# A hybrid decoder layer on one core: the opening's adaLN product in eight strips of one feature slice each

## The chip, the core and the metric

The kernel runs on 1 core of one Trainium2 chip. The metric is the time of one execution on the device, in microseconds (us). Before the change three runs took 726.54, 726.90 and 729.52 us: median 726.9 us.

## The reference

One decoder layer for 512 tokens of width 1024, all float32. What matters here is its start, up to the first products with the normalised input:

```python
mod = silu(c) @ w_ada + b_ada                  # w_ada (1024, 6*1024)
sh_m, sc_m, gt_m, sh_f, sc_f, gt_f = split(mod, 6)
h = rmsnorm(x, norm_pre_mix) * (1.0 + sc_m) + sh_m
proj = h @ w_in                                # HGRN2 q, f, i, g | attention q, k, v | indexer q, k, w
o_hg  = hgrn2_mixer(...)                       # gated recurrence, 4 heads
o_att = dsa_mixer(...)                         # rotary on q, k, q_idx, k_idx (angles from positions),
                                               # indexer scores -> top-k keys -> attention
y = concat(o_hg, o_att) @ w_out
x = x + gt_m * rmsnorm(y, norm_post_mix)
# then a SwiGLU block with its own rmsnorm, shift, scale and gate
```

## The kernel before

Matrices that are multiplied are kept as two parts, a high part rounded to a shorter format (`w_hi`, `h_hi`) and the rest (`w_lo`, `h_lo`). A product is three matmuls: high by high, low by high, high by low. ScalarE writes the high parts (`split_hi`, line 462), VectorE subtracts to get the low parts (`split_lo`, line 817). Every engine has its own list of instructions in the order in which the code is written, and waits on semaphores; nothing is scheduled by a planner. So the order of lines in each engine's block is the order of work.

The opening runs in these steps.

- x comes in four tiles of 128 tokens (`xr`, which the profile shows as res). ScalarE squares a tile and sums it (line 482), takes Ln and Exp (lines 485, 488) to get `rstd`; VectorE scales the tile (`norm_rows`, line 856); TensorE transposes it in 8 pieces (line 1427); ScalarE and VectorE copy one half each out of PSUM into `xt`, features on the partitions (lines 509, 928; the profile shows `xt` as mix).
- `xt` has eight feature slices of 128 features by 512 tokens. Slice k needs the shift and the scale of its 128 features: columns of `silu(c) @ w_ada`. They are computed in four pairs. For a pair TensorE multiplies `silu_pad` with 1024 rows by 512 columns of `w_ada` (`start_ada`, two halves of 4 matmuls, line 1406; each half is a buffer of its own in `start_slot`, shown as adaw or act). ScalarE copies the result out (`copy_rows`, line 528), TensorE sums and turns it into columns with four matmuls by ones (`start_sums`, line 1443), VectorE adds the bias and forms the scale (`start_mods`, lines 953 and 958).
- With them VectorE applies scale and shift to the pair's two slices (`feature_in`, line 965), ScalarE writes `h_hi` (`split_h`, line 532), VectorE `h_lo` (`feature_lo`, line 969).
- TensorE then multiplies the slice with the 584 indexer columns of `w_in`: 10 matmuls that need `h_hi` (`idx_high`, line 1456) and 5 that need `h_lo` (`idx_low`, line 1464). Their accumulation runs over all eight slices in five banks, so the indexer's results are there when slice 7 is done. A pair's `start_ada` stands ahead of the odd slice before it, and its `start_sums` after 4 of that slice's 10 high matmuls.
- Beside it VectorE computes the rotary angles (`angles`, lines 862 to 876): 1 conversion and twice 13 instructions of 128x512, one kind after pair 0, the other after pair 1, each in one piece. ScalarE takes the sines (line 538).

SyncE issues all DMAs, in the order c, x, the first two `w_ada` buffers, the small parameters, slice 0 of the indexer weights, positions, and so on. After the opening follow the HGRN2 and attention heads, the output projection and the feed-forward block, which the change doesn't touch.

## Time and profile before

| | |
|---|---|
| median of 3 runs | 726.9 us (726.54 to 729.52) |
| profiled execution, own time | 728.42 us |
| its span | 726.7 us |
| TensorE matmul busy | 705.7 us, 97% |
| VectorE busy | 434.0 us, 60% |
| ScalarE busy | 296.2 us, 41% |
| GpSimd busy | 11.1 us, 2% |
| mean granted TensorE clock | 0.991 |

The profiled execution's own time is 1.7 us over its span and 1.5 us over the median. Times in the rows are microseconds from the start of the span. A row of the timeline gives start, duration, engine, line, operation, output and inputs with their shapes, the number merged into the row, and in brackets how long the engine was idle before and what ended that. The matmul of the table is pipelined, its ends are modelled.

### The profile page before, as it was taken

The numbers are of one execution on the slowest core, as the hardware profiler recorded it, in microseconds if no ns is written. First come the engines' busy times: TensorE is split into PE (matmuls) and PEld (weight loads), VectorE is DVE, ScalarE is ACT, GpSimd is POOL, SyncE is SP. The second block draws the span as 40 slices with busy tenths as digits, with TensorE's granted clock in tenths as the row PEclk, the third lists the DMA queues.
The fourth block names the chain that finished last, engine by engine and source line by source line (L and its number), as shares of the span: only waits on it lengthen the run. The fifth ranks groups of instructions, "written<-read, shape, count | busy, mean of one in ns | idle before, by whom it ended". The sixth has DMA issues, their size and how long they took to land.

```text
span 726.7 us, 11020 instructions
## 1 busy us (share of the span) xinstructions
PE 705.7 (97%) x3962; PEld 552.7 (76%) x3962; DVE 434.0 (60%) x806; ACT 296.2 (41%) x472; POOL 11.1 (2%) x39
## 2 busy tenths in 40 slices
PE   5999999999999999999999999999999999999997
PEld 4565567777766878878888888888888788888885
DVE  3966678898898999968643433323432335443444
ACT  6445553535454444536572343342343332211223
POOL 4000000000000000000000000000000000000000
PEclk9999999999999999999899999999999999999999
DMA  9944023231222766567225532355533224223202
GB/s 314 358 144 114 3 59 85 62 116 53 62 60 87 217 217 223 182 209 205 81 59 145 144 105 78 106 144 144 144 94 108 87 87 132 99 87 102 71 0 117
DMA packets 95995, 89.10 MB, mean 123 GB/s; under 512 B 2950, under 2 KB 84954, under 8 KB 95964
## 3 DMA queue, kind: packets, MB, share of 16 engines
q1 hardware_dynamic: 95964, 88.70, 39.9%
q8 instruction: 18, 0.29, 0.2%
q14 instruction: 13, 0.11, 0.0%
HBM read 86.59 MB, written 2.10 MB: 122 GB/s over the span
## 4 chain that ended last, share of the span: by engine, by line
PE 61%; DVE 4%; issue 1%; ACT 0%; DVEq 0%; ACTq 0%
PE ps L1342 34%; PE ps L1363 17%; PE ps L1381 6%; DVE rope L892 1%; PE ps L1646 1%; PE ps L1402 1%; PE ps L1529 1%; DVE w_lo L817 1%; PE ps L1666 1%; PE ps L1778 1%; PE ps L1782 1%; PE ps L1779 1%; PE ps L1523 0%; DVE act L1149 0%; DVE res L1154 0%
## 5 line engine op out<-in xcount | busy, mean ns | idle before, releaser
L1342 PE MATMUL ps<-h_hi,w_hi 128*128 128x512 f32 x560 | 227.3, 406 | 0.0
L1342 PE MATMUL ps<-h_hi,w_lo 128*128 128x512 f32 x560 | 218.7, 391 | 0.0
L1342 PE MATMUL ps<-h_lo,w_hi 128*128 128x512 f32 x560 | 218.3, 390 | 0.0
L817 DVE TENSOR_TENSOR w_lo<-w_raw,w_hi 128x1024 fp32r<-128x1024 f32 (+1 forms) x109 | 129.3, 1187 | 99.4 <-ACT w_hi L462 98.9
L462 ACT ACTIVATE w_hi<-w_raw 128x1024 fp32r<-128x1024 f32 (+1 forms) x109 | 111.6, 1029 | 105.9 <-PE ps L1363 86.3
L1342 PEld LDWEIGHTS ps<-h_hi,w_hi 128*128 128x128 f32 x560 | 105.2, 188 | 30.3 <-issue 9.1
L1342 PEld LDWEIGHTS ps<-h_hi,w_lo 128*128 128x128 f32 x560 | 105.1, 188 | 22.6
L1342 PEld LDWEIGHTS ps<-h_lo,w_hi 128*128 128x128 f32 x560 | 105.3, 188 | 20.7 <-issue 1.0
L1363 PE MATMUL ps<-w_hi,h_hi 128*128 128x512 f32 x176 | 70.1, 398 | 0.8 <-DVE mix L1214 0.8
L1363 PE MATMUL ps<-w_hi,h_lo 128*128 128x512 f32 x176 | 68.6, 390 | 0.0
L1363 PE MATMUL ps<-w_lo,h_hi 128*128 128x512 f32 x176 | 68.5, 389 | 0.0
L794 ACT ACTIVATE adaw<-ps 128x512 f32<-128x512 f32 x22 | 13.2, 598 | 132.0 <-PE ps L1342 130.2
L1272 DVE TENSOR_TENSOR act<-adaw,ps 128x512 f32 (+1 forms) x22 | 15.1, 687 | 57.2 <-PE ps L1342 57.2
L1295 DVE CAST h_hi<-act 128x512 fp32r (+1 forms) x22 | 9.4, 426 | 56.8 <-PE ps L1363 53.7
L1363 PEld LDWEIGHTS ps<-w_hi,h_hi 128*128 128x128 f32 x176 | 33.0, 188 | 8.3 <-DVE mix L1214 1.0
L1363 PEld LDWEIGHTS ps<-w_lo,h_hi 128*128 128x128 f32 x176 | 33.1, 188 | 7.2 <-issue 0.5
L1363 PEld LDWEIGHTS ps<-w_hi,h_lo 128*128 128x128 f32 x176 | 33.0, 188 | 6.9
L1075 DVE MAX8 top<-score 128x8 f32<-128x256 f32 (+2 forms) x48 | 25.2, 552 | 6.1 <-PE ps L1590 5.8
L1080 DVE MATCH_REPLACE8 score<-top,score 128x256 f32<-128x256 f32 (+2 forms) x48 | 25.8, 543 | 0.0
L1381 PE MATMUL ps<-w_hi,h_hi 128*128 128x512 f32 x64 | 24.9, 389 | 0.0
L1381 PE MATMUL ps<-w_lo,h_hi 128*128 128x512 f32 x64 | 24.9, 389 | 0.0
L1381 PE MATMUL ps<-w_hi,h_lo 128*128 128x512 f32 x64 | 24.9, 389 | 0.0
(250 smaller groups left out, 791.9 us busy)
## 6 DMA issues: line engine op xcount, KB each, us to landing
w_raw<-in_w_ffn_in SPq DMA_DIRECT2D x44, 512.0 KB, 5.7
w_raw<-in_w_in SPq DMA_DIRECT2D x28, 512.0 KB, 3.8
w_raw<-in_w_ffn_out SPq DMA_DIRECT2D x22, 512.0 KB, 3.5
adaw<-in_w_ada SPq DMA_DIRECT2D x12, 512.0 KB, 3.9
act<-in_w_ada SPq DMA_DIRECT2D x12, 512.0 KB, 9.2
adaw<-in_w_ada SPq DMA_DIRECT2D x6, 1024.0 KB, 5.3
act<-in_w_ada SPq DMA_DIRECT2D x6, 1024.0 KB, 5.1
res<-in_x SPq DMA_DIRECT2D x8, 512.0 KB, 4.7
```

What stands on the lines that cost most here:

```text
L462: sc.activation(w_hi[slot][:, 0:n], w_raw[slot][:, 0:n], ACT.Copy).then_inc(hi_ok, 1)
L794: sc.activation(silu_g[u // 2], ps[u][:, :], ACT.Silu).then_inc(silu_done[u // 2], 1)
L817: V.tensor_tensor(w_lo[slot][:, 0:n], w_raw[slot][:, 0:n], w_hi[slot][:, 0:n].bitcast(f32), ALU.subtract).then_inc(lo_ok, 1)
L892: V.scalar_tensor_tensor(out=total, in0=w, scalar=silu, in1=total, op0=ALU.mult, op1=ALU.add).then_inc(sum_used, 1)
L1075: V.max(top8[:, 8 * (t - 1):8 * t], sc_t[t]).then_inc(top_max, 1)
L1080: V.match_replace(out=sc_t[t], in_to_replace=top8[:, 8 * (t - 1):8 * t], in_values=sc_t[t], imm_value=TAKEN).then_inc(top_rep, 1)
L1272: V.tensor_tensor(act[:, ds(i * 2 * SEQ + v * SEQ, SEQ)], silu_g[v], ps[2 * v + 1][:, :], ALU.mult).then_inc(act_ok[v], 1)
L1295: V.tensor_copy(h_hi[:, at], act[:, ds(k * SEQ, SEQ)]).then_inc(xs_hi, 1)
L1342: last = mm(ps[bank][0:rows, :], a, b, start=(k == 0 and n == 0), stop=(k == KT - 1 and n == 2))
L1363: last = mm(ps[2 * t + b][:, :], a, w, start=(first and n == 0), stop=(last_one and n == 2))
L1381: last = mm(ps[2 * t + b][:, :], a, w, start=False, stop=(n == 3 and m == 2))
L1402: return nc.tensor.transpose(ps[k][:, t * P:(t + 1) * P], xn[:, t * D_MODEL + k * P:t * D_MODEL + (k + 1) * P], ident[:, :])
```

## The change

- The adaLN product of the opening goes in eight strips of one slice (256 columns: 128 of the shift, 128 of the scale) in place of four of two slices (512 columns). Each strip has one buffer, loaded by two DMAs of 128x8x128 (before: four DMAs of 128x4x256 in two buffers for a pair).
- Strips 1 to 3 are multiplied, and their columns summed, within the high matmuls of the slice before. From strip 4 on a strip is multiplied after the low matmuls of the slice two before it, and its columns are summed after four high matmuls of the slice before it.
- VectorE: `start_mods` and `feature_in` for one slice at a time, `feature_lo` of a slice ahead of `split_lo` of the next weights, the angles in quarters of 4, 3, 4 and 2 instructions behind them, over slices 0 to 5.
- The sum of squares of the last x tile goes from ScalarE to VectorE, between the copy of tile 0 and `norm_rows` of tile 2; the columns of tile 1 are copied after `norm_rows` of tile 3.
- ScalarE: `copy_rows` behind `split_idx` of the same slice; sines in slices 4 and 6.
- SyncE: small parameters ahead of `w_ada`, then strips and indexer weights in turn; the key norm's two vectors last, with a semaphore of their own.
- TensorE transposes the small parameters between x tiles 2 and 3.

```diff
-ADA_COLS = 512
+ADA_COLS = 256
             def load_start_ada(n):
-                pair, half = n // 2, n % 2
-                slot = start_slot[n].rearrange("p (k n) -> p k n", k=4)
+                slot = start_slot[n].rearrange("p (k n) -> p k n", k=KT)
                 for a, col in enumerate((0, D_MODEL)):
...
+                    sp.dma_start(slot[:, :, a * P:(a + 1) * P],
+                                 w_ada[0].rearrange("(k p) n -> p k n", p=P)[:, :, col + n * P:col + (n + 1) * P]
                                  ).then_inc(start_loaded[n], 16)
...
             sp.wait_ge(xt_mm, 2 * TT)
...
+            for n in range(4, KT):
+                if n >= 6:
+                    sp.wait_ge(ada_used, n - 5)
                 load_start_ada(n)
+                sp.wait_ge(lo_ok, n - 3)
+                load_idx(n)
...
+                if not seen and t == TT - 1:
+                    sc.wait_ge(xsq_ok, 1)
+                    sc.sem_inc(ss_ok, 1)
+                else:
+                    sc.activation(junk_rows if seen else junk_x, xr[:, t * D_MODEL:(t + 1) * D_MODEL], ACT.Square,
+                                  accum_out=ss[:, t:t + 1]).then_inc(ss_ok, 1)
...
+            copy_rows(0)
+            split_idx(0)
+            for k in range(KT):
+                split_h(k)
+                if k < KT - 1:
+                    split_idx(k + 1)
+                    copy_rows(k + 1)
+                if k in (4, 6):
+                    sines(1 if k == 4 else 0)
...
             norm_rows(0, 0)
             norm_rows(0, 1)
             copy_xt_high(0)
+            ve.wait_ge(x_loaded[TT - 1], 16)
+            V.tensor_tensor_reduce(out=junk_last, in0=xr[:, (TT - 1) * D_MODEL:TT * D_MODEL],
+                                   in1=xr[:, (TT - 1) * D_MODEL:TT * D_MODEL], scale=1.0, scalar=0.0, op0=ALU.mult,
+                                   op1=ALU.add, accum_out=ss[:, TT - 1:TT]).then_inc(xsq_ok, 1)
             norm_rows(0, 2)
-            copy_xt_high(1)
             norm_rows(0, 3)
-            copy_xt_high(2)
-            copy_xt_high(3)
+            for t in range(1, TT):
+                copy_xt_high(t)
...
-            for pair in range(4):
-                start_mods(pair)
-                feature_in(2 * pair)
-                feature_in(2 * pair + 1)
-                feature_lo(2 * pair)
-                split_lo(2 * pair + 1, (2 * pair + 1) % 4, IDX_COLS)
-                feature_lo(2 * pair + 1)
...
+            for k in range(KT):
+                start_mods(k)
+                feature_in(k)
+                if k == 0:
+                    split_lo(0, 0, IDX_COLS)
+                feature_lo(k)
+                if k < KT - 1:
+                    split_lo(k + 1, (k + 1) % 4, IDX_COLS)
+                if k == 0:
+                    ve.wait_ge(pos_loaded, 32)
                     astep(V.tensor_copy(pos, pos_i[:, :].bitcast(i32)))
...
+                for n in ((0,), (1,), (2,), (3, 4), (5,), (6, 7), (), ())[k]:
+                    angles(1 - n // 4, n % 4)
...
+            for k in range(KT):
+                idx_high(k, IDX_ORDER[:2])
+                if k < 3:
+                    start_ada(k + 1)
+                    idx_high(k, IDX_ORDER[2:4])
+                    start_sums(k + 1)
+                    idx_high(k, IDX_ORDER[4:])
+                else:
+                    if k < KT - 1:
+                        start_sums(k + 1)
+                    idx_high(k, IDX_ORDER[2:])
+                idx_low(k)
+                if 2 <= k < KT - 2:
+                    start_ada(k + 2)
```

On VectorE, from the last x tiles on, before the change (line numbers of the kernel before; act is the scaled tile, mix the transposed x):

```order
L856 TENSOR_SCALAR act<-res,rstd 128x1024 [waits rstd_ok]
L928 COPY mix<-ps 128x4x128 [waits xt_mm]
L856 TENSOR_SCALAR act<-res,rstd 128x1024 [waits rstd_ok]
L928 COPY mix<-ps 128x4x128 [waits xt_mm]
L856 TENSOR_SCALAR act<-res,rstd 128x1024 [waits rstd_ok]
L928 COPY mix<-ps 128x4x128 [waits xt_mm] x2
L940 COPY prm<-ps 128x76 [waits prm_mm]
```

The same place after the change (line numbers of the changed kernel):

```order
L852 TENSOR_SCALAR act<-res,rstd 128x1024 [waits rstd_ok]
L924 COPY mix<-ps 128x4x128 [waits xt_mm]
L931 ISA rope,ss<-res 128x1024 [waits x_loaded3]
L931 ISA ss 128x1
L852 TENSOR_SCALAR act<-res,rstd 128x1024 [waits rstd_ok] x2
L924 COPY mix<-ps 128x4x128 [waits xt_mm] x3
L939 COPY prm<-ps 128x76 [waits prm_mm]
```

The square of tile 3 (two instructions, L931) now stands ahead of the scaling of tile 2.

VectorE's work on pair 1 before the change, from the pair's columns to its first angles (score is the angles' buffer):

```order
L953 TENSOR_TENSOR mod<-ps,prm 128x2x2 [waits start_cols]
L958 SCALAR_TENSOR_TENSOR scale_mix<-mod,prm 128x2 [waits start_mod]
L965 TENSOR_SCALAR mix<-mix,scale_mix,mod 128x512 [waits start_scale]
L965 TENSOR_SCALAR mix<-mix,scale_mix,mod 128x512
L969 TENSOR_TENSOR h_lo<-mix,h_hi 128x512 [waits hhi_ok]
L817 TENSOR_TENSOR w_lo<-w_raw,w_hi 128x584 [waits hi_ok]
L969 TENSOR_TENSOR h_lo<-mix,h_hi 128x512 [waits hhi_ok]
L862 TENSOR_SCALAR score<-gate_ffn,rc 128x512
L863 TENSOR_SCALAR score<-score 128x512 [waits ang_step]
```

Slice 2 after the change, up to the columns of slice 3 (bias is the other angles' buffer):

```order
L950 TENSOR_TENSOR mod<-ps,prm 128x2 [waits start_cols,ang_step]
L954 SCALAR_TENSOR_TENSOR scale_mix<-mod,prm 128x1 [waits start_mod]
L961 TENSOR_SCALAR mix<-mix,scale_mix,mod 128x512 [waits start_scale]
L965 TENSOR_TENSOR h_lo<-mix,h_hi 128x512 [waits hhi_ok]
L813 TENSOR_TENSOR w_lo<-w_raw,w_hi 128x584 [waits hi_ok]
L866 TENSOR_SCALAR bias<-bias 128x512
L867 TENSOR_SCALAR act<-bias 128x512 [waits ang_step]
L868 TENSOR_TENSOR bias<-bias,act 128x512 [waits ang_step]
L869 TENSOR_SCALAR bias<-bias 128x512 [waits ang_step]
L950 TENSOR_TENSOR mod<-ps,prm 128x2 [waits start_cols,ang_step]
```

Each slice now has its own wait for columns, and nothing stands between the scaling of a slice and the subtraction that waits for its high part.

TensorE after the change, from slice 0 to the end of its matmuls (L1446 and L1454 are the indexer's high and low matmuls, L1398 a strip's product, L1433 its sums):

```order
L1446 MATMUL ps<-h_hi,w_hi 72x512 [waits hhi_ok,lo_ok]
L1446 MATMUL ps<-h_hi,w_lo 72x512
L1446 MATMUL ps<-h_hi,w_hi 128x512
L1446 MATMUL ps<-h_hi,w_lo 128x512
L1398 MATMUL ps<-act,silu_pad 32x256 [waits start_loaded1,start_rows]
L1398 MATMUL ps<-act,silu_pad 32x256 x7
L1446 MATMUL ps<-h_hi,w_hi 128x512
L1446 MATMUL ps<-h_hi,w_lo 128x512
L1446 MATMUL ps<-h_hi,w_hi 128x512
L1446 MATMUL ps<-h_hi,w_lo 128x512
L1433 MATMUL ps<-ones,ada_rows 128x1 [waits start_mod,start_rows]
L1433 MATMUL ps<-ones,ada_rows 128x1
```

Slice 0 had no such pieces before: its 15 matmuls ran through, and the next strip pair stood behind them.

## Rows read from the trace of the kernel before

**Rows 1.** Timeline of the opening: VectorE's `start_mods` of the four pairs.

```profile
17.98 0.16 DVE L953 TENSOR_TENSOR mod<-ps,prm 128x4 f32<-128x4 f32 x1
...
29.81 0.15 DVE L953 TENSOR_TENSOR mod<-ps,prm 128x4 f32<-128x4 f32 x1
...
41.20 0.15 DVE L953 TENSOR_TENSOR mod<-ps,prm 128x4 f32<-128x4 f32 x1
...
50.34 0.16 DVE L953 TENSOR_TENSOR mod<-ps,prm 128x4 f32<-128x4 f32 x1 [4.01 <-PE ps L1443]
```

**Rows 2.** Timeline: first matmul of slices 0, 4, 6 and 7 on TensorE.

```profile
19.72 0.42 PE L1456 MATMUL ps<-h_hi,w_hi 128*72 128x512 f32 x1 [1.88 <-ACT h_hi L532]
...
42.94 0.42 PE L1456 MATMUL ps<-h_hi,w_hi 128*72 128x512 f32 x1 [1.39 <-ACT h_hi L532]
...
52.78 0.40 PE L1456 MATMUL ps<-h_hi,w_hi 128*72 128x512 f32 x1
...
56.23 0.39 PE L1456 MATMUL ps<-h_hi,w_hi 128*72 128x512 f32 x1
```

**Rows 3.** Windows: busy us of each engine, granted clock, DMA share, GB/s.

```profile
20.50:21.50 1.00, 1.00 (x4) 0.74 (x3) 1.00 (x3) 0.18 (x1) 0.00 (x0) 0.50 1.11 348
...
46.00:47.00 1.00, 1.00 (x11) 0.33 (x13) 0.32 (x1) 0.00 (x0) 0.00 (x0) 1.00 1.02 297
...
355.00:360.00 5.00, 4.71 (x29) 4.47 (x27) 1.54 (x3) 1.18 (x2) 0.00 (x0) 0.68 0.36 105
```

**Rows 4.** Timeline of x: VectorE's scaling of tile 2, the end of ScalarE's square.

```profile
10.04 0.75 DVE L856 TENSOR_SCALAR act<-res,rstd 128x1024 f32<-128x1024 f32 x1
...
11.03 0.19 ACT L482 ACTIVATION_READ_ACCUMULATOR res<-res 128x1 f32 x1
```

**Rows 5.** Timeline: TensorE's transposes, copy and sums of strip pair 0.

```profile
7.42 6.69 PE L1427 MATMUL ps<-ident,act 128*128 128x128 f32 x32 [4.88 <-DVE act L856]
...
16.07 0.60 ACT L528 ACTIVATE ada_rows<-ps 128x512 f32<-128x512 f32 x1 [1.76 <-PE ps L1406]
...
16.82 1.02 PE L1443 MATMUL ps<-ones,ada_rows 128*128 128x1 f32 x8 [0.59 <-ACT ada_rows L528]
```

**Rows 6.** Groups of instructions up to 60 us, by shape: busy us, mean ns.

```profile
L817 DVE TENSOR_TENSOR w_lo<-w_raw,w_hi 128x1024 fp32r<-128x1024 f32 x2 | 2.4, 1221 | 1.5 <-ACT w_hi L462 1.5
```

**Rows 7.** Timeline of VectorE: low parts of slices 4 and 5, weights between.

```profile
42.82 0.69 DVE L969 TENSOR_TENSOR h_lo<-mix,h_hi 128x512 fp32r<-128x512 f32 x1 [0.24 <-ACT h_hi L532]
...
43.43 0.76 DVE L817 TENSOR_TENSOR w_lo<-w_raw,w_hi 128x584 fp32r<-128x584 f32 x1
...
44.11 0.69 DVE L969 TENSOR_TENSOR h_lo<-mix,h_hi 128x512 fp32r<-128x512 f32 x1
```

**Rows 8.** Timeline of VectorE: conversion, first instruction of each angle quarter, next `split_lo`.

```profile
21.50 0.42 DVE L981 CAST gate_ffn<-gate_ffn 128x512 f32<-128x512 int32 x1
...
21.95 0.49 DVE L862 TENSOR_SCALAR bias<-gate_ffn,rc 128x512 f32<-128x512 f32 x1
...
23.86 2.14 DVE L867 SCALAR_TENSOR_TENSOR bias<-bias 128x512 f32<-128x512 f32 x3
...
26.04 0.43 DVE L870 TENSOR_SCALAR bias<-bias 128x512 f32<-128x512 f32 x1
...
28.15 0.48 DVE L875 TENSOR_SCALAR bias<-bias,rc 128x512 f32<-128x512 f32 x1
...
29.13 0.77 DVE L817 TENSOR_TENSOR w_lo<-w_raw,w_hi 128x584 fp32r<-128x584 f32 x1
```

**Rows 9.** Timeline of TensorE: strip pair 3 and the high matmuls around its sums.

```profile
46.51 1.06 PE L1406 MATMUL ps<-adaw,silu_pad 128*32 128x512 f32 x8
...
48.36 0.45 PE L1456 MATMUL ps<-h_hi,w_hi 128*72 128x512 f32 x1
...
49.35 0.95 PE L1443 MATMUL ps<-ones,ada_rows 128*128 128x1 f32 x8
...
50.16 0.49 PE L1456 MATMUL ps<-h_hi,w_hi 128*128 128x512 f32 x1
```

More of the change, by code:

```diff
@@ L133, in build @@
         xt = part(mix, 0, KT * SEQ)
-        junk_x = part(res, 4096, 1024)
+        junk_x, junk_last = part(res, 4096, 1024), part(rope, 0, 1024)
         h32 = [part(act, n) for n in (4096, 4608, 9728, 10752)]
@@ L857, in norm_rows, with angles @@
                                 rstd[:, t:t + 1], None, ALU.mult).then_inc(xn_ok, 1)
-            def angles(kind, second_half):
+            def angles(kind, quarter):
                 a, turns = ang[2 * kind + 1], ang[2 * kind]
-                if not second_half:
+                if quarter == 0:
                     astep(V.tensor_scalar(a, pos, rc[:, 2 * kind:2 * kind + 1], None, ALU.mult))
@@ L945, in _, with start_mods @@
             V.tensor_copy(hpv[:, :, 2], prm[:, C_ONORM:C_ONORM + 4])
-            split_lo(0, 0, IDX_COLS)
             ve.wait_ge(xt_low, TT)
             ve.wait_ge(xt_high, TT)
-            def start_mods(pair):
-                ve.wait_ge(start_cols, pair + 1)
-                two = slice(2 * pair, 2 * pair + 2)
-                V.tensor_tensor(mod[:, 0:16].rearrange("p (a j) -> p a j", a=2)[:, :, two],
-                                ps[6][:, 0:4].rearrange("p (a j) -> p a j", a=2),
-                                prm[:, 0:16].rearrange("p (a j) -> p a j", a=2)[:, :, two],
+            def start_mods(k):
+                ve.wait_ge(start_cols, k + 1)
+                V.tensor_tensor(mod[:, 0:16].rearrange("p (a j) -> p a j", a=2)[:, :, k],
+                                ps[6][:, 0:2], prm[:, 0:16].rearrange("p (a j) -> p a j", a=2)[:, :, k],
                                 ALU.add).then_inc(start_mod, 1)
-                ve.wait_ge(start_mod, pair + 1)
-                V.scalar_tensor_tensor(out=scale_mix[:, two], in0=mod[:, 8 + 2 * pair:10 + 2 * pair], scalar=1.0,
-                                       in1=prm[:, C_PRE_MIX + 2 * pair:C_PRE_MIX + 2 * pair + 2], op0=ALU.add,
+                ve.wait_ge(start_mod, k + 1)
+                V.scalar_tensor_tensor(out=scale_mix[:, k:k + 1], in0=mod[:, 8 + k:9 + k], scalar=1.0,
+                                       in1=prm[:, C_PRE_MIX + k:C_PRE_MIX + k + 1], op0=ALU.add,
                                        op1=ALU.mult).then_inc(start_scale, 1)
-                ve.wait_ge(start_scale, pair + 1)
+                ve.wait_ge(start_scale, k + 1)
             def feature_in(k):
@@ L1029, in _ @@
             ve.wait_ge(idx_ok, 5)
+            ve.wait_ge(sin_ok, 4)
             n = 0
@@ L1405, in ada_mm @@
             def ada_mm(bank, strip, k, w, first, last_one):
-                return mm(ps[bank][strip * 32:(strip + 1) * 32, :], silu_pad[:, k * 32:(k + 1) * 32], w, start=first,
-                          stop=last_one)
-            def ada_half(bank, half, w):
-                for strip in range(4):
-                    last = ada_mm(bank, strip, 4 * half + strip, w[:, strip * ADA_COLS:(strip + 1) * ADA_COLS],
-                                  half == 0, half == 1)
-                last.then_inc(ada_used, 1)
+                return mm(ps[bank][strip * 32:(strip + 1) * 32, 0:ADA_COLS], silu_pad[:, k * 32:(k + 1) * 32], w,
+                          start=first, stop=last_one)
             te.wait_ge(c_loaded, 16)
@@ L1420, in _ @@
                 if t == 3:
+                    te.wait_ge(prm_loaded, 16 * 5)
+                    nc.tensor.transpose(ps[6][:, KT:KT + N_PRM], prm_rows[0:N_PRM, :],
+                                        ident[0:N_PRM, 0:N_PRM]).then_inc(prm_mm, 1)
                     te.wait_ge(xt_low, 1)
@@ L1430, in _, with start_ada, start_sums @@
             te.wait_ge(silu_ok, 1)
-            def start_ada(pair):
-                if pair:
-                    te.wait_ge(start_rows, pair)
-                for half in range(2):
-                    te.wait_ge(start_loaded[2 * pair + half], 32)
-                    ada_half(7, half, start_slot[2 * pair + half])
-            def start_sums(pair):
-                te.wait_ge(start_rows, pair + 1)
-                if pair:
-                    te.wait_ge(start_mod, pair)
-                for q in range(4):
+            def start_ada(n):
+                if n:
+                    te.wait_ge(start_rows, n)
+                te.wait_ge(start_loaded[n], 32)
+                for k in range(KT):
+                    last = ada_mm(7, k % 4, k, start_slot[n][:, k * ADA_COLS:(k + 1) * ADA_COLS], k < 4, k >= 4)
+                last.then_inc(ada_used, 1)
+            def start_sums(n):
+                te.wait_ge(start_rows, n + 1)
+                if n:
+                    te.wait_ge(start_mod, n)
+                for q in range(2):
                     last = mm(ps[6][:, q:q + 1], ada_rows[:, q * P:(q + 1) * P], ones[:, 0:1], start=True, stop=True)
```

99 lines of the change are left out of this document (26 added, 73 removed).

## The prediction, made before the changed kernel ran

> **What bounds the kernel now.** I first took the busy shares of the page: TensorE 97% of the span. So a change in the opening is worth what it moves the end of the opening; behind it TensorE has no slack that would take a shift up. Then I read the timeline up to 60 us. The opening's end is the indexer's last matmul of slice 7: its first is at 56.23, the slice takes 3.45 (56.23 less 52.78), so it ends at 59.7 [rows 2].
>
> What sets the pace inside is seen by VectorE's `start_mods` [rows 1]. Pair 1 and pair 2 start theirs at 29.81 and 41.20 with no idle time in brackets: the columns had been there, VectorE was late. Only pair 3's waits, 4.01 us for TensorE. So VectorE paces the first two pairs (11.83 and 11.39 us), TensorE the last two (9.14 us to the next `start_mods`). Where VectorE paces, TensorE waits: 1.39 us before slice 4 [rows 2]. The cause is the angles: 13 instructions in one piece ahead of the next weights' low part and the next columns.
>
> [...]
>
> **The front, to the first columns.** Before: columns of pair 0 at 17.98 [rows 1], slice 0 on TensorE 1.74 us later [rows 2].
>
> The square of x tile 3 on VectorE stands where tile 2's scaling began, at 10.04 [rows 4]. No row shows this instruction. Its nearest row is a subtraction of the same size with two inputs, 1.22 us [rows 6]; a lower bound is a pass with one input, 0.75 [rows 4], an upper one twice the subtraction, 2.4. I take 1.2, and 0.15 for reading the accumulator (ScalarE's read takes 0.19 [rows 4]): 1.35. So tile 2 is scaled at 11.39, done at 12.14. Before, TensorE ran its 32 transposes without a gap from 7.42 in 6.69 us, 0.21 each [rows 5]: tile 2 began at 7.42 + 16 x 0.21 = 10.8. Now it begins at 12.2, 1.4 later, tile 3 behind it and the parameters' transpose (0.2), and x is transposed at about 15.8 instead of 14.1. ScalarE, which is relieved, was not late: nothing is won there.
>
> [...]
>
> Strip 0 against that: before, the pair's copy began at 16.07 [rows 5]. A strip takes 0.95 (half of a pair's 1.85, 48.36 less 46.51 [rows 9]): 15.85 to 16.8, copy at 16.9. The copy is half as long (0.38 for 0.60), the sums are two matmuls for four (0.5 for 1.02 [rows 5]). Before it was 1.91 from copy to columns; now 1.91 - 0.22 - 0.5 = 1.2: columns at 18.1. `start_mods` and one scaling pass take the same, and `split_lo` of weights 0, which now stands in the time that VectorE waits for the high part, ends 1.72 after the columns. Slice 0 starts at 18.1 + 1.75 = 19.85, against 19.72. The smaller strip pays for the square, no more.
>
> **VectorE's pace.** From columns to the first low part 1.62 us (42.82 less 41.20 [rows 1, 7]), as before, since it is a chain over ScalarE. Low part to weights 0.61, weights to the next 0.68 [rows 7]. So a slice without angles takes 2.93 us. The quarters of the angles take 1.91, 2.18, 2.11 and 0.98, the conversion 0.45 [rows 8]. From columns to readiness for the next:
> - slice 0: 2.93 + 0.45 + 1.91 = 5.3
> - slice 1: 2.93 + 2.18 = 5.1
> - slice 2: 2.93 + 2.11 = 5.05
> - slice 3: 2.93 + 0.98 + 1.91 = 5.8
> - slice 4: 5.1
> - slice 5: 2.93 + 2.11 + 0.98 = 6.0
>
> Together 32.4 us for six slices. Before, the same stretch (pair 0 to pair 3) took 50.34 - 17.98 = 32.4 [rows 1]. The work is the same; the waits for the high part are now one of some 0.7 us per slice instead of one of 0.24 per pair [rows 7]; that eats what the spreading gives.
>
> **TensorE's pace.** A slice 3.45 [rows 2], a strip 0.95, its sums 0.41 (half of 50.16 - 49.35 [rows 9]): 4.8 us a slice, 5.8 for slice 2, which has two strips. VectorE needs 5.1 to 6.0, so it paces most of the way. Columns k+1 come at the earliest 3.3 us after slice k starts for k below 3 (8 high matmuls of 0.23, strip, sums, 0.13), 1.5 after it later. The slice starts 1.7 after its columns.
>
> The slow clock now hurts: strip 1 and its sums stand inside slice 0. With half speed for 3.4 us, as the trace has it (20.3 to 23.7), columns 1 come at 19.85 + 3.3 + 1.6 = 24.8, though VectorE is ready at 23.4. Then columns: 24.8, 29.9, 34.95, 40.8, 45.9, 51.9 for slices 1 to 6. Slices start at 26.5, 31.6, 37.4 (TensorE, two strips), 42.5, 47.6, 53.6. Slice 7 has no angles before it: 53.6 + 3.45 + 0.41 = 57.5. End at 61.0, against 59.7: 1.3 later.
>
> **Transfers.** Rows of `w_ada` become 512 bytes. The loads of 512-byte rows behind the opening reach 297 GB/s with the DMA engines full, against 348 for the 1 KB rows [rows 3]. The strips' 8.39 MB (16 loads of 512 KB) take 28.3 us in place of 24.1, 4.2 more. Eight loads one after the other, strip 1 with its weights is in by about 17, strip 7 and weights 7 by about 44; they are needed at 20.8 and 52. Hidden. So are SyncE's waits: `lo_ok` for weights 4 is given at about 19.8, while the queue still works on strips 3 and 4. The sines end before the rotations that wait for them, as angles end at about 51.9.
>
> **Sum.** +0.1 front, +1.5 slow clock now exposed, about -0.3 in the last slices: +1.3. On the profiled execution 728.42 gives 729.7; that execution was 1.5 over the median, so against the median 726.9 + 1.3 = 728.2.
>
> **Rivals.**
> - The slow stretch doesn't fall on strip 1. The chip gave half speed after an idle TensorE in one place of the opening; a run may have it elsewhere or not. Then columns 1 come at 23.4 and all is 1.4 to 1.5 earlier: end 59.5, 726.7 us. For it: the idle time before slice 0 hardly changes, so the place can shift by a little. Against: the same idle time is there. [...]
> - TensorE alone paces: VectorE's instructions pack closer than I count, and the square is hidden. Then slice 0 starts at 19.72 less half a strip pair (0.95), half the copy (0.22) and half the sums (0.5): 18.0. Eight slices, seven strips and sums are 8 x 3.45 + 7 x 1.36 = 37.1; with 1.7 for the clock the end is 56.8, 2.9 earlier: 724.0. Without the slow clock 722.3. For it: TensorE's waits before go. Against: the pace of pairs 0 and 1.
> - Slower: the slow clock holds twice as long. In 355 to 360 the mean clock is 0.68 [rows 3], a second stretch with small matmuls around it; strips of 8 short matmuls and sums of 2 between slices are of that sort. A further 1.7 us, and with a square of 2.4 us 1.2 more: 728.2 + 2.9 = 731.1. [...]
> - Transfers set the pace. It would need a rate at which strip 7 lands after 52 us, below about 220 GB/s; the 297 speaks against it. At 200 GB/s it would land 3.8 later (42.0 us for 38.1), and the time would be 732.0.
>
> **How the numbers follow.** Main case 0.50 (726.9 to 729.5), no slow clock on strip 1 0.24, TensorE's pace 0.13, longer slow clock 0.10, transfers 0.03. 0.5% (3.6 us) is about what a measurement of this kernel tells from no change: below 723.3 or above 730.5. Faster takes half of the third case: 0.07. Slower takes most of the last two: 0.09. The rest, 0.84, is the same. The range reaches from the third case to just short of the fourth: 724.0 to 730.8.
>
> **What would show it.** Right: the square at about 10.0 lasting 1.2 with a gap in the transposes; columns 0 near 18.1; no idle time before VectorE's `start_mods` of slices 2 to 6; an idle TensorE before slices 4 to 6; end of slice 7 near 61. Wrong: `start_mods` waiting for TensorE in slices 2 to 6, intervals under 5 us, strips waiting for DMA, or a slice 0 before 19.

## The result, and the profile after

Over 20 runs the changed kernel took 729.74 us (median), the kernel before 727.88 in 20 runs of its own. The ratio is 1.0025, 95% interval [1.0014, 1.0035]: slower by 1.8 us, inside the range and on the side that was forecast (+1.3). The profiled execution took 729.72 us with a span of 727.9. Three executions far off the others stand in no ratio: 3988.18 us among these 20 of the kernel before, 1009.14 in e1, and 791.80 of the kernel before beside e1 to e4. The same kernel in a later set of 12 runs gave 1.0005 [0.9987, 1.0023]; the two intervals overlap, and what the spread goes with is below.

The opening in the timeline of the changed kernel, VectorE's `start_mods` (line 950 here) of slices 0 to 4, 6 and 7:

```profile
16.41 0.16 DVE L950 TENSOR_TENSOR mod<-ps,prm 128x2 f32<-128x2 f32 x1 [1.16 <-PE ps L1433]
...
23.42 0.16 DVE L950 TENSOR_TENSOR mod<-ps,prm 128x2 f32<-128x2 f32 x1 [1.02 <-PE ps L1433]
...
28.87 0.16 DVE L950 TENSOR_TENSOR mod<-ps,prm 128x2 f32<-128x2 f32 x1 [0.39 <-PE ps L1433]
...
34.31 0.16 DVE L950 TENSOR_TENSOR mod<-ps,prm 128x2 f32<-128x2 f32 x1 [0.45 <-PE ps L1433]
...
40.12 0.16 DVE L950 TENSOR_TENSOR mod<-ps,prm 128x2 f32<-128x2 f32 x1
...
51.22 0.16 DVE L950 TENSOR_TENSOR mod<-ps,prm 128x2 f32<-128x2 f32 x1
...
54.47 0.16 DVE L950 TENSOR_TENSOR mod<-ps,prm 128x2 f32<-128x2 f32 x1 [0.25 <-PE ps L1433]
```

The first columns are there 1.6 us earlier than before (17.98 [rows 1]); slices 1 to 3 wait for TensorE, slices 4 and 6 find their columns ready: VectorE is late there. The same timeline on TensorE, slices 0, 6 and 7:

```profile
18.15 0.55 PE L1446 MATMUL ps<-h_hi,w_hi 128*72 128x512 f32 x1 [1.88 <-DVE w_lo L813]
...
52.97 0.43 PE L1446 MATMUL ps<-h_hi,w_hi 128*72 128x512 f32 x1 [0.88 <-ACT h_hi L530]
...
57.28 0.42 PE L1446 MATMUL ps<-h_hi,w_hi 128*72 128x512 f32 x1 [0.22 <-ACT h_hi L530]
...
59.61 1.32 PE L1454 MATMUL ps<-h_lo,w_hi 128*72 128x512 f32 x5
```

Slice 7 starts at 57.28 against 56.23 [rows 2]. The last of its 15 matmuls starts at 60.54 (59.47 before), so with 0.23 for it the opening ends at 60.8 against 59.7. Behind it hardly anything is added: the heads' first matmul stands at 65.89 (before 64.69), and the span is 1.2 longer too. The change's effect is in the opening.

**Two parts of the opening.** The opening is split here at the first columns. In the four profiles of the changed kernel's order the stretch behind them came out the same to 0.2 us, and in the three of the order before to 0.1, however late the first columns were; in all seven the clock stood at half speed, a granted clock of 0.50, for 3.4 us around slice 0. Where that differs, so does the stretch: e6, e11 and e12 have one order there and show 39.9, 43.4 and 41.4. The time of the first columns came out anywhere within 3.3 us. The last two columns split once more, at the start of slice 1, when the slow stretch is over in each profile of the table but e2, which has more of them:

| profiled kernel | first columns | end of slice 7 | between | slice 1 starts | from there to the end |
|---|---|---|---|---|---|
| before | 17.98 | 59.70 | 41.7 | 26.74 | 33.0 |
| changed | 16.41 | 60.77 | 44.4 | 25.17 | 35.6 |
| changed, profiled again (e8) | 18.80 | 63.01 | 44.2 | 27.39 | 35.6 |
| changed, square on ScalarE (e3) | 16.49 | 60.82 | 44.3 | 25.23 | 35.6 |
| changed, warmed (e9) | 17.87 | 62.20 | 44.3 | 26.58 | 35.6 |
| before, square on VectorE (e4) | 19.74 | 61.50 | 41.8 | 28.48 | 33.0 |
| before, warmed (e10) | 19.27 | 61.01 | 41.7 | 27.94 | 33.1 |
| before, angles spread (e7) | 18.26 | 60.35 | 42.1 | 28.10 | 32.3 |
| changed, angles in one piece (e2) | 18.36 | 75.62 | 57.3 | 28.28 | 47.3 |
| changed, wait filled (e1) | 19.23 | 62.21 | 43.0 | 27.72 | 34.5 |
| changed, strips ahead (e5) | 16.68 | 59.25 | 42.6 | 25.73 | 33.5 |
| strips ahead and wait filled (e6) | 18.66 | 58.53 | 39.9 | 25.71 | 32.8 |
| e6, warmed (e11) | 17.05 | 60.41 | 43.4 | 27.55 | 32.9 |
| e6, warmed, square on ScalarE (e12) | 18.12 | 59.50 | 41.4 | 26.66 | 32.8 |

(The end is the start of slice 7's last matmul in the timeline plus 0.23.) So the new order costs 2.6 us behind the first columns. The 20 runs say 1.8 in all; the front then gives back some 0.8 in the mean, which is a difference and not seen directly.

Where the 2.6 us lie is seen from slice start to slice start on TensorE, two slices at a time:

| | before | changed | more |
|---|---|---|---|
| slices 0 and 1 | 11.84 | 12.47 | 0.63 |
| slices 2 and 3 | 11.38 | 11.30 | -0.08 |
| slices 4 and 5 | 9.84 | 11.05 | 1.21 |
| slices 6 and 7 | 6.92 | 7.80 | 0.88 |

In slices 0 to 3 VectorE was slow before too, so little is lost there. Slices 4 to 7 are where TensorE alone set the pace before. Now it waits 0.88 us in front of slice 6 and 0.22 in front of slice 7, a slice with its strip and sums takes it 5.05 us where it was 4.92 (half of 9.84), and the last sums stand in slice 6, where before no such work was left.

**The slow clock and the whole time.** The mean granted clock of an execution says how much of it ran at half speed: the profile of before has 0.50 for 3.4 us from 20.3, for 6.8 from 351.4 and for the last 3.2, and 0.991 in the mean (1 less 13.4 x 0.5 / 726.7). The runs of the changed kernel (these 20 and the 12 of e8) against those of the kernel before that have this figure (three sets, 98 runs):

| mean granted clock | changed, mean us (runs) | before, mean us (runs) | more |
|---|---|---|---|
| 0.997 to 1.000 | 726.57 (7) | 725.94 (16) | 0.6 |
| 0.993 and 0.994 | 729.95 (18) | 727.37 (33) | 2.6 |
| 0.988 to 0.992 | 730.33 (7) | 728.87 (49) | 1.5 |

Where hardly any slow stretch fell, the new order costs little (0.6 us); most of its cost goes with the slow clock (2.6 and 1.5). The sets were not all run on one chip, and the table does not say which slow stretch does it.

### The profile page after: what moved, and what is told of

Read it like the earlier page. It is cut to its first block, busy times and chain, and to the rows that moved or that the text cites. A ratio compares the mean times of both kernels' runs of the same rounds, so it can differ in the third digit from the quotient of the medians.

```text
span 727.9 us, 11178 instructions
## 1 busy us (share of the span) xinstructions
PE 706.2 (97%) x4026; PEld 552.9 (76%) x4026; DVE 437.6 (60%) x816; ACT 295.8 (41%) x474; POOL 11.8 (2%) x39
## 4 chain that ended last, share of the span: by engine, by line
PE 64%; DVE 2%; issue 0%; DVEq 0%; ACT 0%
PE ps L1334 35%; PE ps L1355 17%; PE ps L1373 6%; PE ps L1655 1%; PE ps L1635 1%; PE ps L1394 1%; PE ps L1518 1%; PE ps L1767 1%; PE ps L1771 1%; PE ps L1768 1%; PE ps L1512 0%; PE ps L1648 0%; DVE w_lo L813 0%; DVE act L914 0%; DVE act L1141 0%
## 5 line engine op out<-in xcount | busy, mean ns | idle before, releaser
L1264 DVE TENSOR_TENSOR act<-adaw,ps 128x512 f32 (+1 forms) x22 | 15.1, 687 | 57.3 <-PE ps L1334 57.3
L1355 PEld LDWEIGHTS ps<-w_hi,h_hi 128*128 128x128 f32 x176 | 33.1, 188 | 8.2 <-DVE mix L1206 1.0
L1355 PEld LDWEIGHTS ps<-w_lo,h_hi 128*128 128x128 f32 x176 | 33.1, 188 | 7.2 <-issue 0.5
L1355 PEld LDWEIGHTS ps<-w_hi,h_lo 128*128 128x128 f32 x176 | 33.1, 188 | 7.0
L1072 DVE MATCH_REPLACE8 score<-top,score 128x256 f32<-128x256 f32 (+2 forms) x48 | 25.8, 543 | 0.0
```

The source lines that it names most:

```text
L1072: V.match_replace(out=sc_t[t], in_to_replace=top8[:, 8 * (t - 1):8 * t], in_values=sc_t[t], imm_value=TAKEN).then_inc(top_rep, 1)
L1264: V.tensor_tensor(act[:, ds(i * 2 * SEQ + v * SEQ, SEQ)], silu_g[v], ps[2 * v + 1][:, :], ALU.mult).then_inc(act_ok[v], 1)
L1355: last = mm(ps[2 * t + b][:, :], a, w, start=(first and n == 0), stop=(last_one and n == 2))
```

## The experiments

Three theories stood against each other. A is the prediction's: VectorE sets the pace of slices 1 to 6, and a slow stretch of the clock comes to lie where TensorE is the bound. B was formed on reading the trace after: in slices 0 to 2 a loop over three engines sets the pace, from the slice over the next strip, its copy, its sums and its columns to the high part of the next slice. C says that the clock's level in the front decides when all of it starts. All runs are timed in 5 rounds against the kernel before; "columns" are the rows and sums that `start_mods` reads.

**e1: VectorE's wait filled.**

```diff
 # VectorE, slice k of 1 to 6 (ScalarE: split_idx(k + 1) ahead of split_h(k))
                 feature_in(k)
-                feature_lo(k)
-                split_lo(k + 1, ...)
+                split_lo(k + 1, ...)
+                feature_lo(k)
```

> The changed kernel, with the low part of the next weights put into VectorE's wait for the high part of the slice (slices 1 to 6; ScalarE splits those weights first). Theory A (the prediction's: VectorE's order paces slices 1 to 6, 0.70 us of each spent waiting for the high part): the intervals between columns shrink by about 0.7 us each until TensorE paces, the opening ends 2 to 3 us earlier, about 727 us, ratio to before near 0.999. Theory B (the trace of the changed kernel shows VectorE late only for slice 6, by 0.88; slices 1 and 2 go round a loop strip, copy, sums, columns, high part): only that 0.9 us comes back, ratio near 1.001, and the columns of slices 2 and 3 still come 5.4 us after the ones before.

Ratio 1.0006 [0.9994, 1.0018] in 11 runs. Slices 2 and 3 on VectorE, timeline:

```profile
31.42 0.16 DVE L953 TENSOR_TENSOR mod<-ps,prm 128x2 f32<-128x2 f32 x1 [1.06 <-PE ps L1438]
31.62 0.16 DVE L957 SCALAR_TENSOR_TENSOR scale_mix<-mod,prm 128x1 f32<-128x1 f32 x1
31.81 0.55 DVE L964 TENSOR_SCALAR mix<-mix,scale_mix,mod 128x512 f32<-128x512 f32 x1
32.27 0.77 DVE L816 TENSOR_TENSOR w_lo<-w_raw,w_hi 128x584 fp32r<-128x584 f32 x1
33.06 0.69 DVE L968 TENSOR_TENSOR h_lo<-mix,h_hi 128x512 fp32r<-128x512 f32 x1
...
36.86 0.16 DVE L953 TENSOR_TENSOR mod<-ps,prm 128x2 f32<-128x2 f32 x1 [1.12 <-PE ps L1438]
```

The wait for the high part is gone from the slice, and the columns still come 5.44 us after the ones before: VectorE now waits 1.12 us for them instead of 0.45. In slices 1 and 2 it did not set the pace. Columns to end fell from 44.3 to 43.0, most of it at slice 6, which TensorE no longer waits for. That is theory B. In the whole time the gain is not clear of noise: the changed kernel itself measured 1.0025 and 1.0005.

**e2: the angles in one piece again.**

```diff
-                for n in ((0,), (1,), (2,), (3, 4), (5,), (6, 7), (), ())[k]:
+                for n in ((), (0, 1, 2, 3), (), (4, 5, 6, 7), (), (), (), ())[k]:
```

> The changed kernel with the angles of each kind in one piece again, one behind slice 1, one behind slice 3. If VectorE's order can pace the opening, the columns of slice 2 come 10.6 us after those of slice 1 and those of slice 4 10.1 us after those of slice 3; the opening ends 8 to 9 us later, ratio to before about 1.014. If TensorE alone paces (the rival), within 1 us of the changed kernel.

Ratio 1.0178 [1.0159, 1.0197] in 5 runs, against some 1.014 expected: 13 us over the kernel before. Between columns and end the profile shows 57.3 us, 12.9 more than the changed kernel's, where 8 to 9 were expected. TensorE's waits in the timeline:

```profile
38.84 0.67 PE L1446 MATMUL ps<-h_hi,w_hi 128*72 128x512 f32 x1 [5.22 <-ACT h_hi L530]
...
56.33 0.42 PE L1446 MATMUL ps<-h_hi,w_hi 128*72 128x512 f32 x1 [4.09 <-ACT h_hi L530]
```

The columns of slices 2 and 4 came at 37.09 and 54.59, 10.56 and 10.10 us after the ones before them, as expected. The rest goes with the clock, as far as one profile tells: the trace gives half speed for 6.8 us from 19.5, 6.8 from 36.5 and 3.4 from 57.0, the last two in or right behind those waits. So VectorE can set the pace, and with single strips it must be relieved: with pairs the same pieces cost far less (waits of 0.26 and 1.39 us before slices 2 and 4 in the kernel before).

**e3 and e4: the square of tile 3, undone in the changed kernel and done alone in the one before.**

```diff
 # e3, in the changed kernel (e4 does the reverse in the kernel before)
-            V.tensor_tensor_reduce(out=junk_last, ...).then_inc(xsq_ok, 1)
             norm_rows(0, 2)
+            copy_xt_high(1)
             norm_rows(0, 3)
-            for t in range(1, TT):
-                copy_xt_high(t)
+            copy_xt_high(2)
+            copy_xt_high(3)
...
 # and ScalarE squares tile 3 like the others
-                if not seen and t == TT - 1:
+                if False:
                     sc.wait_ge(xsq_ok, 1)
```

> The changed kernel with the square of x tile 3 on ScalarE again and the copies of the tiles in their old places. The prediction's front: tile 2 is scaled 1.35 us earlier, the transposes run without a gap, and the first columns come 1.4 us earlier: ratio to before about 1.0005. Rival: transposes behind the gap take 0.11 us each in the changed kernel and 0.21 without it, so the gap costs nothing, first columns within 0.3 us of 16.4, ratio unchanged at 1.0025.

> The kernel before with only the square of x tile 3 on VectorE, and the copies of the tiles behind it. The prediction's front: first columns at 19.4 instead of 18.0, and since VectorE paces from there all is 1.4 us later, ratio 1.002. Rival (the gap in the transposes is made up by faster transposes): first columns within 0.3 us of 18.0, ratio 1.000.

e3: 0.9999 [0.9982, 1.0016], e4: 1.0002 [0.9988, 1.0017]. e4's interval leaves out the 1.002 of the prediction by little. e3's takes in the prediction's 1.0005 and leaves out the rival's 1.0025, but the unaltered kernel itself gave 1.0005 later (e8), so that decides nothing. The two profiles tell more. e3's first columns are at 16.49, the changed kernel's at 16.41: no cost. e4's are at 19.74, 1.76 after those of before: a cost, though not the gap alone. TensorE's idle time ahead of tile 2 is 0.96 us of it; the rest goes with the level, which rose 2.6 us later than in the kernel before. What differs between the two comparisons is the clock. TensorE in the front, first of the changed kernel, then of the same kernel profiled again (e8):

```profile
7.41 3.68 PE L1416 MATMUL ps<-ident,act 128*128 128x128 f32 x16 [4.71 <-DVE act L852]
...
12.05 1.10 PE L1416 MATMUL ps<-ident,act 128*128 128x128 f32 x8 [0.97 <-DVE act L852]
...
13.06 1.04 PE L1416 MATMUL ps<-ident,act 128*128 128x128 f32 x8
```

```profile
7.41 3.68 PE L1416 MATMUL ps<-ident,act 128*128 128x128 f32 x16 [4.91 <-DVE act L852]
12.33 1.97 PE L1416 MATMUL ps<-ident,act 128*128 128x128 f32 x8 [1.24 <-DVE act L852]
...
14.22 1.91 PE L1416 MATMUL ps<-ident,act 128*128 128x128 f32 x8
```

The starts of the transposes are 0.109 us apart in the one and 0.213 in the other, and from tile 2's first to tile 3's first it is 1.01 us against 1.89: two levels. e9 shows both at one step of the clock records, from 1.00 to 0.50 at 13.1: the transposes of tile 2, ahead of it, start 0.109 us apart, the last of tile 3's, behind it, 0.213. The trace's clock records put the rise to full speed at 11.5 in the first, 16.8 in the second, 13.5 in the kernel before, 16.1 in e4. Ahead of the first record the windows print 1.00, though the transposes' spacing of 0.213 us shows the low level. With the same program the first columns came 2.4 us apart; 0.28 of that is there before tile 2 is transposed, whose start moved from 12.05 to 12.33, and the rest is read as the level's. At the low level the transposes behind the square's gap didn't make it up: in e4 they stay 0.213 us apart, and the strips start at 15.66 where they started at 14.04 before. At the high level they did, and ScalarE's square saves nothing: in e3 tile 3 is scaled only at 12.21, waiting 0.39 us for ScalarE, and its transposes start at 13.14 where the changed kernel's start at 13.06. This rests on four single profiles.

**e5 and e6: strips one place ahead; the same with VectorE's wait filled.**

```diff
 # TensorE, e5
             start_sums(0)
+            start_ada(1)
             for k in range(KT):
                 idx_high(k, IDX_ORDER[:2])
-                if k < 3:
-                    start_ada(k + 1)
-                    ...
+                if k < KT - 1:
+                    start_sums(k + 1)
+                idx_high(k, IDX_ORDER[2:])
                 idx_low(k)
-                if 2 <= k < KT - 2:
+                if k < KT - 2:
                     start_ada(k + 2)
 # e6: also e1's edit
```

> The changed kernel with every strip one place ahead on TensorE: strip 1 between the sums of strip 0 and slice 0 (in TensorE's wait), strip k+2 behind the low matmuls of slice k from slice 0 on; sums after four high matmuls as before. Theory B (slices 0 to 2 go round the loop strip, copy, sums, columns, high part, 5.45 us a round, where VectorE needs 5.1 and TensorE 4.9): columns of slices 2 and 3 come 5.1 us after the ones before, VectorE paces from there; the opening ends about 2 us before the changed kernel's, ratio to before near 1.000. Theory A (the prediction's: VectorE paces those slices anyway, only strip 1 in the slow clock is exposed): about 1 us earlier than the changed kernel, ratio 1.001.

> Strips one place ahead and the low part of the next weights in VectorE's wait for the high part. If loop and VectorE's wait are the two things that hold TensorE, no idle time of TensorE is left between slices 1 and 7 and a slice takes about 4.9 us: from first columns to the end of the opening some 40 us against 44.4 in the changed kernel and 41.7 before; ratio to before 0.996 to 0.998. If the slow clock decides, it stays near 1.000.

e5: 0.9994 [0.9980, 1.0009]; e6: 0.9973 [0.9958, 0.9989], 12 runs each. The loop inside a slice is best seen in the changed kernel, slice 1, timeline of three engines: slice, strip, copy, sums, columns, high part, next slice.

```profile
25.17 0.42 PE L1446 MATMUL ps<-h_hi,w_hi 128*72 128x512 f32 x1
...
26.21 1.07 PE L1398 MATMUL ps<-act,silu_pad 128*32 128x256 f32 x16
27.21 0.51 PE L1446 MATMUL ps<-h_hi,w_hi 128*128 128x512 f32 x1
...
27.35 0.38 ACT L526 ACTIVATE ada_rows<-ps 128x256 f32<-128x256 f32 x1 [1.75 <-PE ps L1398]
...
28.26 0.50 PE L1433 MATMUL ps<-ones,ada_rows 128*128 128x1 f32 x4
...
28.87 0.16 DVE L950 TENSOR_TENSOR mod<-ps,prm 128x2 f32<-128x2 f32 x1 [0.39 <-PE ps L1433]
...
29.84 0.63 ACT L530 ACTIVATE h_hi<-mix 128x512 fp32r<-128x512 f32 x1 [2.11 <-DVE mix L961]
...
30.62 0.42 PE L1446 MATMUL ps<-h_hi,w_hi 128*72 128x512 f32 x1
```

From slice to columns 3.70 us, from columns to slice 1.75: a round of 5.45. With the strips ahead (e5) the columns of slices 2 and 3 come at 27.77 and 32.79 after 22.67, rounds of 5.10 and 5.02, VectorE's pace, with no idle time in front of them:

```profile
22.67 0.16 DVE L950 TENSOR_TENSOR mod<-ps,prm 128x2 f32<-128x2 f32 x1
...
27.77 0.16 DVE L950 TENSOR_TENSOR mod<-ps,prm 128x2 f32<-128x2 f32 x1
...
32.79 0.16 DVE L950 TENSOR_TENSOR mod<-ps,prm 128x2 f32<-128x2 f32 x1
```

It cost one thing back: strip 1 was not there in TensorE's wait ahead of slice 0, which then started 1.7 us late (e5, timeline of TensorE):

```profile
18.24 1.93 PE L1398 MATMUL ps<-act,silu_pad 128*32 128x256 f32 x16 [1.70 <-DMA act<-in_w_ada]
...
51.44 0.42 PE L1446 MATMUL ps<-h_hi,w_hi 128*72 128x512 f32 x1 [0.41 <-ACT h_hi L530]
```

The second row shows what e5 leaves: VectorE is still late for slice 6. In e6 TensorE has no wait over 0.25 us left behind slice 0, and slices 1 to 5 take 5.0 to 5.1 us each. Its 39.9 us from columns to end are helped by chance: the clock stayed at full speed there. The same order in the loop took 41.4 in e12, with 3.4 us of half speed and TensorE waiting 0.86 us for strip 1, and 43.4 in e11, with 6.8 us and 1.97: between 1 and 4.5 us less than the changed kernel. From the start of slice 1 on all three show 32.8 to 32.9, where the changed kernel has 35.6 (1.0 of that is one strip, which now stands ahead of slice 0) and the kernel before 33.0. So the two edits together take back the whole 2.6 us that the new order had cost there (35.6 less 33.0). In the whole time e6 measured 2.0 us less than the kernel before, e11 1.5 less (0.9980) and e12 the same (1.0002); that this order beats the kernel before is likely and not certain.

**e7: the angles spread in the kernel before.**

```diff
                 if pair < 3:
                     split_lo(2 * pair + 2, (2 * pair + 2) % 4, IDX_COLS)
+                for n in ((0, 1), (2, 3, 4), (5, 6, 7), ())[pair]:
+                    angles(1 - n // 4, n % 4)
```

> The kernel before with pairs and strips of 512 columns as they were; only the angles are cut in quarters and go behind the next weights' low part: two quarters in pair 0, three in pair 1, three in pair 2, sines in pairs 2 and 3. If the angles in one piece cost TensorE its waits before slices 2 and 4 and the strips in pairs cost nothing, the opening ends 1.5 to 2 us earlier than before, ratio 0.9975. If spreading is worth nothing, 1.000.

1.0005 [0.9991, 1.0019]: no gain. The test was not clean. With the angles behind it `split_lo` met its wait for the high weights in the open, in pair 2 for 2.18 us:

```profile
39.93 0.16 DVE L953 TENSOR_TENSOR mod<-ps,prm 128x4 f32<-128x4 f32 x1 [0.40 <-PE ps L1438]
...
45.72 0.77 DVE L817 TENSOR_TENSOR w_lo<-w_raw,w_hi 128x584 fp32r<-128x584 f32 x1 [2.18 <-ACT w_hi L462]
```

and this profile had a slow stretch of 6.8 us at slice 0 (18.9 to 25.8). What spreading is worth with pairs stays open.

**e8: the changed kernel again.**

> The changed kernel unaltered, on the same chip as the others of this set, so that they can be compared with it: ratio to before 1.0025 as before, and by both theories the same chain, whatever the first columns' time: 44.0 to 44.8 us from first columns to the end of slice 7 unless the slow stretch lies elsewhere.

1.0005 [0.9987, 1.0023], 725.59 to 731.86 us; the profiled execution was the slowest of them. Between columns and end 44.2 us, as expected.

**e9 to e12: TensorE warmed.** 22 transposes of the identity into a free bank, whose results nothing reads, stand ahead of the x tiles, in the changed kernel (e9), the kernel before (e10), e6 (e11), and e6 with e3's edit (e12).

```diff
             nc.tensor.transpose(ps[6][:, 0:KT], c_rows[:, :], ident[0:KT, 0:KT]).then_inc(c_mm, 1)
+            for n in range(22):
+                nc.tensor.transpose(ps[7][:, 0:P], ident[:, :], ident[:, :])
```

> The changed kernel with 22 transposes of the identity into a free bank ahead of the first x tile, in TensorE's 4.8 us of waiting (2.6 to 7.4). Theory C (the transposes of x run at 0.213 us at the chip's low level and 0.107 at the high one, and where the level rises moves the first columns between 16.4 and 18.8): with the extra work the level is high before tile 2, first columns at 16.3 to 16.8, no run above 730, mean about 1 us lower than the changed kernel's 729, ratio to before near 1.000. Rival (the front is set by x and its squares, the clock is chance): nothing changes.

> The kernel before with the same 22 transposes. Theory C: the transposes of x no longer run without a gap, x is transposed at about 13.6, but strip pair 0 still waits for its second buffer (14.9), so first columns only 0 to 0.5 us earlier than 17.98; then VectorE paces, ratio to before 0.999 to 1.000. The slow stretch at slice 0 costs it nothing either way.

> Strips one place ahead, next weights' low part in VectorE's wait, and the 22 transposes. Theory C: first columns at 16.4 in place of 18.7, so about 1 us in the mean below the same kernel without them (0.9973): ratio 0.995 to 0.9965. If the front is chance, 0.9973.

> As the one before, with the square of x tile 3 on ScalarE again. With the transposes at 0.107 us they no longer run without a gap, so tile 2, scaled at 10.0 instead of 11.2, is transposed about 1.2 us earlier, but tile 3 can't be scaled before 11.8 to 12.2 either way: first columns within 0.4 us, the same ratio within 0.001. By the prediction's front it would be 1.35 us faster (0.002 less).

Ratios: e9 1.0029 [1.0010, 1.0049], e10 1.0005 [0.9987, 1.0024], e11 0.9980 [0.9962, 0.9997], e12 1.0002 [0.9988, 1.0016]. Warming did what it should to the level: it rose at 5.4 to 7.4 us in the four, and in e9 the transposes of tile 0 and tile 1 are 0.109 us apart (0.107 in the expectations). It gained nothing, and the expectations for e9 to e12 were missed. In e9 TensorE stood idle for 1.91 us ahead of tile 2, and the level fell again at 13.1, and once more at 19.9. VectorE's square of x tile 3 in e9 (run e9_after_warm, timeline of VectorE, 8 to 15 us) starts at 9.79, takes 1.33 us, and has waited 0.32 us for the tile:

```profile
9.79 1.33 DVE L931 CUSTOM_DVE_ANT_0 rope<-res 128x1024 f32<-128x1024 f32 x1 [0.32 <-DMA res<-in_x]
```

The level in the same run, windows of the front (the columns are busy time of TensorE, its weight loads, VectorE, ScalarE and GpSimd, granted clock, DMA share, GB/s):

```profile
13.10:16.50 3.40, 3.40 (x24) 1.79 (x22) 1.82 (x6) 0.72 (x2) 0.00 (x0) 0.50 1.18 302
16.50:19.50 3.00, 0.64 (x8) 0.52 (x4) 1.54 (x4) 1.62 (x4) 0.00 (x0) 1.00 1.09 323
```

That fall is not the whole reason. In e10 the level stayed high from 7.2 to 20.9, all through the front, and the first columns came at 19.27, 1.3 later than without the burst: ScalarE waited 0.51 us for x tile 2, and TensorE for the second half of strip pair 0, which it had at 14.94 before (e10, timeline of TensorE):

```profile
11.41 1.10 PE L1429 MATMUL ps<-ident,act 128*128 128x128 f32 x8 [1.25 <-DVE act L856]
...
16.24 1.06 PE L1406 MATMUL ps<-act,silu_pad 128*32 128x512 f32 x8 [0.78 <-DMA act<-in_w_ada]
```

Theory C is half right: the level sets the speed of the transposes (0.109 or 0.213 us from one to the next), but this burst ahead of them moved nothing forward, and the landing of x and of the strips is a second source of spread (VectorE waited 0.32 us for x tile 3 in e9, 1.16 in e11, 1.20 in e1, not at all in the changed kernel). e12 against e11 says once more that the square on ScalarE is not faster; its ratio is even the higher one, with intervals that overlap.

## Why the prediction was right

- **What bounds the opening.** Right: VectorE paced the first pairs before, TensorE waited, and the end of slice 7 carries through to the end. Too wide for the changed kernel: of slices 1 to 6 only the last started by VectorE's lateness.
- **The front, +0.1.** In the profile it was -1.6. The steps that failed are "0.21 each" for the transposes, taken as a fixed cost where it was the low level (0.109 at the high one), and with it "x is transposed at about 15.8": it was 13.9. The square itself took 1.22 us and its read 0.08, with 1.14 from start to the tile behind, against 1.35. In e8, at the low level, the first columns came at 18.8, 0.7 after the forecast; in e4 the columns came 1.8 later, at a level that also rose later. So the forecast holds for one state of the clock and not in the mean.
- **VectorE's pace.** Columns 4, 5 and 6 came 5.81, 5.09 and 6.01 us after the ones before, forecast 5.8, 5.1 and 6.0. TensorE waited 0.88 before slice 6. Before slices 4 and 5 it did not wait (the forecast had it idle there): its own slices were longer, 6.24 with two strips against 5.8, and 5.06 against 4.8. In slices 2 to 4 TensorE set its own pace, which is the second rival's mechanism in part.
- **Slices 1 and 2.** "Columns k+1 come at the earliest 3.3 us after slice k starts" is the term that was mis-sized: it is 3.70, in small pieces, read from the loop's rows in e5's paragraph: the four matmuls ahead of the strip take 1.04 (25.17 to 26.21) and the four between strip and sums 1.05 (27.21 to 28.26), where 0.92 was assumed, since the step from one matmul to the next is 0.23 us within a group and 0.32 to 0.34 next to a strip; the strip takes 1.00, not 0.95, and the sums to the columns 0.61 (28.26 to 28.87), not 0.54. The rounds were 5.45 in place of 5.0 to 5.1, and VectorE's waits for the columns of slices 2 and 3 (0.39 and 0.45) are what the prediction itself had named as a sign of being wrong. e1 and e5 show that this loop was the bound there.
- **The slow clock exposed.** Right in kind: the changed kernel's slow stretch (18.3 to 21.7, windows at 0.50) lay over slice 0 and strip 1, and the first interval was 7.0 us where VectorE needs 5.3. From slice 0 to the columns of slice 1 it took 5.27 us, 1.57 more than the 3.70 at full speed; 1.6 was forecast. Before, the half speed (20.5 to 21.5 [rows 3]) moved nothing that the rows show: the columns of pair 1 were there when VectorE came for them at 29.81 [rows 1]. In the changed kernel VectorE waited 1.02 us for these columns of slice 1, and would have waited 1.66 had it not stood 0.64 for the weights of slice 1 before; 1.4 was forecast (24.8 less 23.4). Those weights came late, with 0.65 us of ScalarE's idle time behind a DMA, but ScalarE then waited 2.57 us for strip 1, so they cost nothing. The table by granted clock says the same of the whole time.
- **Transfers.** 302 to 316 GB/s in windows of 5 us from 25 to 45 against 297 assumed: the size was nearly right. They were hidden, as forecast, though slice 1's weights came later than the 17 that were forecast (split at 18.66).
- **The last slices, -0.3.** The prediction gives no working for this term, and its own times say the opposite: slice 6 with the sums of slice 7 at 3.86 where it took 3.45 before. It took 4.31, so the last slices cost 0.9 and gave nothing. 0.22 of it is TensorE's wait, whose reason is in the last section; the rest is in its own work.
- **The sum.** Forecast +0.1 in front and +1.2 behind; measured 2.6 behind the columns and 1.8 in all. In the profile the first columns came 1.7 us before the forecast's 18.1, and the stretch behind them took 1.5 longer than forecast (7.0, 5.45, 6.24 and 4.31 for slices 0, 1, 2 and 6, forecast 6.65, 5.1, 5.8 and 3.9). Two errors of opposite sign met, so that the profiled executions differ by just 1.3 us is luck; the side was right by mechanism. Against the forecast median of 728.2 the measured 729.74 is 1.5 higher, just above the main case (729.5), and 1.0 of that is the kernel before, whose median of 20 is 727.88 and not 726.9. Of the rivals, none of the four came about as written. The first one's cause, a slow stretch that lies elsewhere or not at all, exists: the runs near full clock are the fast ones.

## What to carry to other kernels

Cutting a producer's step in half doesn't halve the loop that it sits in: from columns to the next slice it took 1.75 us for one slice as for two (1.74), and the copy 0.38 instead of 0.60, so a round here had 5.45 us where TensorE and VectorE each need 5.0 to 5.1, and the cure was to start the producer one round earlier and to put other work into the wait. Smaller pieces also cost TensorE a little each (0.32 to 0.34 us from one matmul to the next beside a strip, 0.23 within a group), and they bring work into slices that had none. Judge such an edit by a stretch between two events that the clock and the loads don't move, with several profiles of one program, and look where the slow clock fell in each; a single profile's end of the opening moved by 2.2 us by itself. And take an instruction's duration with the level that it ran at: a transpose was 0.109 us here or 0.213.
